# The high half of the modulated stream: a VectorE copy becomes a second ScalarE activation from PSUM

## The reference, cut to what matters

```python
def modulate(h, shift, scale):
    return h * (1.0 + scale) + shift

p = modulate(x, sh1, sc1) @ w_in[l]                 # mixer: retention and convolution follow
x = layer_norm(DEEPNORM_ALPHA * x + g1 * mix_x, ln1_w[l], ln1_b[l])
y = jnp.square(jax.nn.relu(modulate(h, shift, scale) @ w1)) @ w2   # MLP
```

## Time and profile before

| | us |
|---|---|
| median of 3 runs | 3218.61 |
| lowest and highest | 3217.91, 3223.07 |
| the profiled execution | 3222.41 |
| its span | 3220.6 |
| PE busy | 2902.3 (90%) |
| DVE busy | 2237.7 (69%) |
| ACT busy | 709.3 (22%) |
| POOL busy | 1036.7 (32%) |

### The profile page before, as it was taken

How to read it: one execution, slowest core, us unless ns; L and a number is a source line. 1 busy time by engine, 2 the same in 40 slices (tenths; PEclk the granted TensorE clock), 3 DMA queues, 4 the chain that set the end, 5 groups by cost and what they waited for, 6 DMA issues and landing times.

```text
span 3220.6 us, 36797 instructions
## 1 busy us (share of the span) xinstructions
PE 2902.3 (90%) x12840; PEld 2268.5 (70%) x12840; DVE 2237.7 (69%) x3490; ACT 709.3 (22%) x1416; POOL 1036.7 (32%) x939
## 2 busy tenths in 40 slices
PE   7798999778699999999997599998797999999994
PEld 1487778347588888888885487784376787777873
DVE  0497675376777786868688787652667778777787
ACT  0322323332311111111111333332323111111111
POOL 0133435165411111111113444462553222222124
PEclk9898999889899999999999799998898999999997
DMA  9311112443011111111112311114421111111111
GB/s 360 73 40 46 48 36 99 138 146 91 26 40 39 39 39 39 39 36 36 35 37 27 104 41 52 56 56 173 132 82 39 53 44 47 46 45 52 39 46 65
DMA packets 256867, 216.06 MB, mean 67 GB/s; under 512 B 60864, under 2 KB 204800, under 8 KB 256768
## 3 DMA queue, kind: packets, MB, share of 16 engines
q10 hardware_dynamic: 143112, 125.89, 12.7%
q1 hardware_dynamic: 113656, 88.93, 9.1%
HBM read 191.62 MB, written 23.17 MB: 67 GB/s over the span
## 4 chain that ended last, share of the span: by engine, by line
PE 75%; DVE 12%; issue 6%; POOL 3%; ACT 2%; DMA 2%; SPq 0%; ACTq 0%; POOLq 0%; DVEq 0%
PE bank L515 12%; PE bank L517 12%; PE bank L516 12%; PE bank L940 8%; PE bank L941 8%; PE bank L942 8%; PE bank L591 5%; PE bank L815 2%; PE bank L816 2%; PE bank L817 2%; DVE work L1565 2%; PE bank L871 1%; PE bank L870 1%; DVE x_hl L1336 1%; PE bank L854 1%
## 5 line engine op out<-in xcount | busy, mean ns | idle before, releaser
L1301 POOL TENSOR_TENSOR w_lo<-raw,w_hi 128x1024 fp32r<-128x1024 f32 x120 | 305.2, 2544 | 1174.8 <-ACT w_hi L1159 1174.8
L1567 DVE TENSOR_TENSOR work<-work 128x512 f32<-128x512 f32 x576 | 555.2, 964 | 20.0
L515 PE MATMUL bank<-w_hi,h_hi 128*128 128x512 f32 x1152 | 458.3, 398 | 43.4 <-DVE work L1565 43.4
L940 PE MATMUL bank<-x_hl,w_hi 128*128 128x512 f32 (+1 forms) x1280 | 474.8, 371 | 2.7 <-ACT work L1150 1.4
L941 PE MATMUL bank<-x_hl,w_hi 128*128 128x512 f32 (+1 forms) x1280 | 472.8, 369 | 0.0
L942 PE MATMUL bank<-x_hl,w_lo 128*128 128x512 f32 (+1 forms) x1280 | 472.3, 369 | 0.0
L517 PE MATMUL bank<-w_hi,h_lo 128*128 128x512 f32 x1152 | 451.7, 392 | 0.0
L516 PE MATMUL bank<-w_lo,h_hi 128*128 128x512 f32 x1152 | 451.5, 392 | 0.0
L1565 DVE TENSOR_TENSOR work<-bank,work 128x512 f32<-128x512 f32 x576 | 393.1, 682 | 0.0
L1466 DVE SCALAR_TENSOR_TENSOR bank<-work,bank 128x512 f32<-128x512 f32 (+1 forms) x580 | 366.5, 696 | 3.9
L1544 DVE TENSOR_TENSOR work<-work 128x512 f32<-128x512 f32 (+1 forms) x160 | 124.9, 781 | 347.3 <-ACT work L1150 347.3
(11 more groups left out here) (131 smaller groups left out, 4451.9 us busy)
## 6 DMA issues: line engine op xcount, KB each, us to landing
raw<-in_w_ff ACTq DMA_DIRECT2D x128, 512.0 KB
plain_words<-in_w_ada SPq DMA_DIRECT2D x12, 2048.0 KB
plain_words<-in_w_ada ACTq DMA_DIRECT2D x12, 2048.0 KB
raw<-in_w_in ACTq DMA_DIRECT2D x64, 256.0 KB
raw<-in_w_in ACTq DMA_DIRECT2D x16, 512.0 KB
raw<-in_w_out ACTq DMA_DIRECT2D x16, 512.0 KB
gate_rows<-work SPq DMA_DIRECT2D x80, 64.0 KB, 1.6
retention_rows<-work SPq DMA_DIRECT2D x72, 64.0 KB, 1.5
```

What stands on the lines that cost most here:

```text
L515: nc.tensor.matmul(out_ps, hi, whi, start=first, stop=False)
L940: nc.tensor.matmul(o, slot(mlp_slot(f), 0)[:, wc], x_hi[:, k, cols], start=k == 0, stop=False)
L1301: nc.gpsimd.tensor_tensor(slot(mlp_slot(sl), 1), raw[:, un % 2, :], slot(mlp_slot(sl), 0).bitcast(F32), ALU.subtract).then_inc(w_ready, 1)
L1567: nc.vector.tensor_tensor(X[:, t, hc], X[:, t, hc], y_t[:, yi % 2, :], ALU.add).then_inc(S["y_add"], 1)
```

## The change

`modulate_step` issues the same activation twice from the same PSUM bank: once into the `mod32` slot and once into `x_hi`, whose type makes the write round. Only the second one reports `mod_in`. `split_step` loses its copy and the wait behind it; the subtraction into `x_lo` stays. The semaphore `hi_in` goes. This holds for all 88 items.

```diff
@@ modulate_step (ScalarE)
                 cd = cond_of(t0)
-                nc.scalar.activation(mod32[:, j % 2, 0:n * P], tr_bank(which, j)[:, 0:n * P], ACT.Identity,
-                                     bias=modc[:, 2 * which, cd, k:k + 1], scale=modc[:, 2 * which + 1, cd, k:k + 1]).then_inc(S["mod_in"], 1)
+                cols = slice(t0 * P, (t0 + n) * P)
+                for dst in (mod32[:, j % 2, 0:n * P], x_hi[:, k, cols]):
+                    last = nc.scalar.activation(dst, tr_bank(which, j)[:, 0:n * P], ACT.Identity,
+                                                bias=modc[:, 2 * which, cd, k:k + 1], scale=modc[:, 2 * which + 1, cd, k:k + 1])
+                last.then_inc(S["mod_in"], 1)
@@ split_step (VectorE)
                 dve.wait_ge(S["mod_in"], s0["mod_in"] + base + j + 1)
-                nc.vector.tensor_copy(x_hi[:, k, cols], m32).then_inc(S["hi_in"], 1)
-                dve.wait_ge(S["hi_in"], s0["hi_in"] + base + j + 1)
                 nc.vector.tensor_tensor(x_lo[:, k, cols], m32, x_hi[:, k, cols].bitcast(F32), ALU.subtract).then_inc(S["split_in"], 1)
```

More of the change, by code:

```diff
@@ L233, in layer_counts @@
         x_in=0 if l else 32, small_in=96, mod2_in=64, conv_in=80, rope_in=32, rows_in=96, gate_in=64, gate2_in=64, cv_st=64,
-        tr_in=t_in + t_mlp, hi_in=t_in + t_mlp, mod_in=t_in + t_mlp, split_in=t_in + t_mlp, gn_aff=2 * n,
+        tr_in=t_in + t_mlp, mod_in=t_in + t_mlp, split_in=t_in + t_mlp, gn_aff=2 * n,
         proj_done=2 * conv_steps + q_tiles, post_evac=q_tiles,
```

## The result

| | before | after |
|---|---|---|
| median of 17 runs each | 3219.19 | 3226.77 |
| lowest and highest | 3213.71, 3227.09 | 3224.36, 3232.41 |
| the profiled execution | 3222.41 | 3224.95 |
| its span | 3220.6 | 3223.1 |
| DVE busy | 2237.7 (69%) | 2199.9 (68%) |

The ratio after to before is 1.0022, 95% interval 1.0014 to 1.0029: the change costs 7.1 us, 4.5 to 9.3. The forecast was +7.0. DVE gave up 38 us of work, ACT took 50 more, and the time went up.

The account below looks back on a forecast made before the run. The prediction took PE to set the time over the whole span. Its terms, 2 x 3.5 ahead of the mixers, - 2 x 1.5 beside the norms, + 2 x 1.5 in the last chunks, gave +7.0 us: 3225.6, range 3217 to 3233.

Parts of the forecast that it names:

- Pitch of a pair: On ACT, 0.665 us from one activation's start to the next, so 1.33 per item against DVE's 1.06 before.
- (a): Ahead of each mixer, up to the first projection step: PE's last transposes wait for item 13, 1.2 us late.
- (b): Items 16 to 19 ahead of each mixer: the transposes of item 19 wait for item 17, 1.3 us more.
- (c): Items 20 to 23 ahead of each mixer, to the end of the last subtraction: 1.0 us more.
- Beside the norms: Items beside each layer's norm: DVE paces and its stalls cover the second activation, -1.5 us per layer.
- turn 6: Beside the first layer's norm, where two POOL instructions hold copy and subtraction: 0.6 us gained.
- turn 11: Beside the first layer's norm: POOL's L1288 comes 0.4 to 0.5 us sooner, item 15's pair ends 0.9 sooner.
- The last chunks: Last chunk of each layer: PE starts the hidden step 1.5 us later, +1.5 each.
- The stalls leave with the copies: Rival: what takes a held copy's place slips in ahead of or behind POOL's instruction; -7.2 us, 3211.4; chance 0.08.
- The ring hides (a): Rival: ACT's idle 2.22 us ahead of item 7 takes up the pairs; +4.6 us without (a), 3223.2; chance 0.20.
- The clock falls: Rival: one PE step falls from 2.4 to 1.2 GHz, 5 us more; +12, 3230.6; chance 0.12 shared with "No overlap".
- No overlap: Rival: a pair writing two tiles does not overlap, pitch 0.78 us; +13.8, 3232.4; chance 0.12 shared with "The clock falls".

Follow-up runs that it names:

- e1: The second activation only for the 48 items ahead of the two mixers, the other 40 keep DVE's copy, against the kernel before: 3224.99 us, ratio 1.0015.
- e2: The second activation only for the 40 items ahead of the MLPs, the others keep DVE's copy, against the kernel before: 3221.36 us, ratio 1.0000.
- e3: The second activation only for the 24 items beside the norms, the rest as in the kernel before: 3218.99 us, ratio 0.9994 to it.
- e9: The second activation only for the 16 items of the two last chunks, the rest as in the kernel before: 3225.06 us, ratio 1.0011 to it.
- e5: The changed kernel with the second activation a plain copy of the bank, without scale and shift: 3219.67 us, ratio 0.9989 to the kernel before.
- e6: The changed kernel with a third activation per item, into x_lo, which the subtraction overwrites: 3271.2 us, ratio 1.0150 to the kernel before.
- e8: The changed kernel with four PSUM banks instead of two ahead of the mixers: 3227.13 us, ratio 1.0014 to the kernel before.
- e7: Pairs only beside the norms and for mixer items 0, 1, 5, 6, 10, 11, 15, the rest as in the kernel before: 3214.17 us, ratio 0.9972.
- e4: The changed kernel with DVE's copy kept beside the second activation for all 88 items: 3243.14 us, ratio 1.0066 to the kernel before.
- e10: The kernel before with four PSUM banks instead of two ahead of the mixers: 3219.69 us, ratio 0.9999 to the kernel before.
- e11: e7 with four PSUM banks instead of two ahead of the mixers: 3211.24 us, ratio 0.9975 to the kernel before.

## Why the prediction was right, step by step

- **Pitch of a pair.** 0.665 us forecast, 0.665 measured. The estimate worked out from the Trainium skill, "ScalarE: Activation LUTs", section "What ACT_TABLE_LOAD costs", was 0.71; the measurement decides, and two activations overlap by some 0.115 us here where the page has 93 ns.
- **(a) Up to the first projection step: right in mechanism and nearly in size.** 1.2 forecast, 1.65 and 1.67 measured (e1: 1.26 and 1.68). Two things that are not the change's account for most of the excess. In the first layer item 7 came 10.76 us behind item 0, against 10.73 before, and not 0.35 sooner. But the weight load ahead of item 5 waited for its transfer and started 6.90 us behind item 0, against 6.54 before; from that load to item 7 it is 3.86 us instead of 4.19, the gain that was forecast. In e1, whose load came at 6.52, item 7 is 0.35 sooner and (a) is 1.26. Timeline of ACT before, then after:

```profile
115.25 1.00 ACT L998 ACTIVATE work<-bank,work 128x256 f32<-128x256 f32 x2
...
121.79 1.06 ACT L495 ACTIVATE w_hi<-raw 128x1024 fp32r<-128x1024 f32 x1 [1.24 <-DMA raw<-in_w_in]
```

```profile
114.96 0.55 ACT L1000 ACTIVATE work<-bank,work 128x256 f32<-128x256 f32 x1
...
121.86 1.06 ACT L495 ACTIVATE w_hi<-raw 128x1024 fp32r<-128x1024 f32 x1 [1.09 <-DMA raw<-in_w_in]
```

In the second layer item 13, counted from item 0, ends 1.31 us later than before; the other 0.36 is PE's. Its last transposes ran at a granted clock of 0.50 after, and of 1.00 in the execution before. Timeline of PE before, then after:

```profile
1817.83 0.66 PE L787 MATMUL bank<-work 128*128 128x128 f32 x4 [0.40 <-ACT work L998]
```

```profile
1819.57 1.11 PE L787 MATMUL bank<-work 128*128 128x128 f32 x4 [0.23 <-ACT x_hl L1000]
```

e2, e3 and e9, which leave the mixer as it was, have 0.50 there as well and +0.33 in (a); their -0.10 to +0.18 in the first layer goes with the same transfer (loads at 6.44 to 6.73). Less these two, (a) is about 1.3 in either layer. The rest followed the forecast: the weight load at 129.29 (129.2 forecast), item 12's pair at 133.44 (133.3), item 13's end at 135.44 + 0.78 = 136.22 (136.1), and PE's last transposes right behind it. That these times of day agree so closely is partly chance, since item 0 had started 0.29 us sooner. Timeline of ACT and of PE after:

```profile
125.72 0.57 ACT L1000 ACTIVATE work<-bank,work 128x256 f32<-128x256 f32 x1 [0.98 <-DVE x_hl L1337]
...
129.29 1.07 ACT L495 ACTIVATE w_hi<-raw 128x1024 fp32r<-128x1024 f32 x1
...
133.44 0.78 ACT L1000 ACTIVATE work<-bank,work 128x512 f32<-128x512 f32 x1 [0.40 <-DVE x_hl L1337]
...
135.44 0.78 ACT L1000 ACTIVATE x_hl<-bank,work 128x512 fp32r<-128x512 f32 x1
```

```profile
136.28 1.12 PE L787 MATMUL bank<-work 128*128 128x128 f32 x4 [0.22 <-ACT x_hl L1000]
137.05 0.56 PE L815 MATMUL bank<-x_hl,w_hi 128*128 128x256 f32 x1
```

- **(b) and (c).** 1.3 and 1.0 forecast; 1.34 and 1.04 in both layers of e1 and in the first of the kernel after. In its second layer (b) is 2.91: PE's step there took 6.83 us instead of 5.58, with a granted clock of 0.69 from 1833 to 1836, where e1 had 1.00 in its own. e5 and e6 moved both terms with ACT's time per item (at 1.14, 1.33 and 2.0 us (b) is 0.97, 1.34 and 2.69). That this is ACT's pace is shown.
- **Beside the norms: the right sign, too large.** -3.0 forecast, -1.87 measured, the same in e2 and e3. L1351 was held 2.29 us, as forecast, and the norm started 0.8 sooner; the stretch with turn 6 gave 0.43 where 0.6 was forecast. In turn 11 the step failed by its POOL term: L1291 came 0.3 sooner, not 0.4 to 0.5, and took 2.77 us, not the 2.52 of the earlier trace rows, so item 15's pair ended 0.46 sooner than before, not 0.9. The second layer repeats this: 0.43 up to the last pair's end and 0.55 by the last split without its copy, 0.98 where 1.5 was forecast. The term for turns 9 to 11 was thus put at twice its size in both layers.
- **The last chunks.** +1.5 forecast for PE's start, +1.56 measured, twice, and in e2, e8 and e9 too. The end of the step moved less, +0.36 and +1.07. The forecast took PE's half clock there as given; but the granted clock of that step rose sooner in the kernel after. By stage, PE's hidden step before and after, and e7's, whose last chunk is that of the kernel before (columns as in the earlier trace rows):

```profile
879.20:886.60 7.40, 7.40 (x26) 6.00 (x26) 4.62 (x9) 3.59 (x5) 2.48 (x1) 0.73 0.26 73
```

```profile
881.30:887.40 6.10, 6.10 (x26) 5.01 (x25) 2.77 (x4) 5.48 (x8) 0.54 (x1) 0.90 0.28 81
```

```profile
873.70:879.90 6.20, 6.20 (x26) 5.11 (x25) 4.58 (x9) 3.56 (x5) 1.71 (x1) 0.89 0.29 83
```

The same 24 passes take 7.4 us at a mean granted clock of 0.73 and 6.2 at 0.9. e7 has the short step without any change there, so the gain need not be the change's.

**The sum.** Forecast 7.0; the stretches of one execution 8.7; the ratio 7.1. The errors of (a) (+0.9, of it 0.7 by the transfer and the clock) and of the norms (+1.1) lie on the same side; the steps' clock took 2.2 back and (b) of the second layer added 1.6. The size of the sum owes something to that luck, its sign does not: (b), (c) and the last chunks' starts came within 0.1 us of the forecast in the kernel after (its second (b) aside), and again in e1, e2 and e9 where these have pairs.

**The rivals.** "The stalls leave with the copies" falls: subtractions and the shift are held, both of the kind that waits for POOL. But it was nearer than its chance of 0.08 says: e7 shows that the copy is worth having gone where POOL works, once the pair is not paid elsewhere. "The ring hides (a)" falls by 1.65 and 1.67, about 1.3 each without the transfer and the clock. "The clock falls" happened in part. In the kernel after one step of the second layer lost 1.6 us by it, with the transposes ahead of it, and not 5; e4 has the same loss in the same place ((b) 2.94, granted clock 0.71 from 1846 to 1848). e1 has the same pairs and no such fall, and none of before, e2, e3 and e9 has one there. Whether pairs bring it on, and what it adds to the median, is not shown. "No overlap" falls by the pitch.

**What stays open.** e7's stretches with changed work hold 4.0 us, its ratio says 9.0 (5.5 to 12.2); e3 shows steps of unchanged code 2.8 us shorter in its one execution while its ratio stands at -1.9. Part of this may be that the profiled execution before had long steps. Whether pairs leave PE a better clock on average is not settled. e10's (a) and (b) come to -6.4 us and its ratio is 0.9999: some 3 us of this come back in the steps behind (a), where PE waits for splits in the second layer; the other 3 are not traced.

## What to carry to other kernels

Moving work from one engine of a pair to the other is priced per place, by who paces that place, and by its time per item: here ACT's 1.33 us against DVE's 1.06, though both engines are far from busy on average. The relief is worth most where another engine holds the relieved one, and the price is paid where nothing does; choosing by item (e7) turned +7 us into -9. Before counting on a relief, look at which instruction stands behind the relieved one, and whether rows show that kind running under the other engine. When a second resource such as PSUM banks is added to cure the wait, look first at which engine sets the pitch: if it is unchanged, the wait only moves.

## What the runs showed of the hardware

- Activations of 128x512 from PSUM with scale and bias columns: 0.78 us alone, 0.665 from start to start, whatever the output (float32 or fp32r). A plain copy of the same size into the same tile: 0.60 and 0.47.
- An instruction of DVE on one column, 0.15 us when free, took 2.29 while POOL worked on 128x1024: the hold does not depend on its size. Statistics (0.64 us each in a pair), a one-column TENSOR_SCALAR (0.15) and an addition with one input in PSUM (0.68) were not held under POOL; a TENSOR_SCALAR of 128x16 (L1363 before) was, once, 2.30 us against 0.18.
- The same hidden step of PE, same code, took from 6.14 to 7.66 us in the first layer's last chunk over executions of kernels that don't change it (before, e1, e3, e7, e10, e11), with a mean granted clock of 0.73 in the first of these and 0.89 in e7. One execution's stretch can't tell a change of 1 us there; the start of the step can.
